# The start offsets of four activation tiles in SBUF

## The reference

```
first block:  x += fox_mixer(rms(x));  x += relu(rms(x) @ up)^2 @ down      (up 1024x4096)
              k, v from rms(x);        x += mla_mixer(rms(x));  x += the same kind of MLP
              x = rms(x)
second block: x += gla_mixer(rms(x));  x += (silu(conv(a)) * conv(u)) @ down  (up 1024x5632)
              x += short_conv_mixer(rms(x));  x += the same kind of MLP
              x = rms(x)
```

## Time and profile before

| | |
|---|---|
| median of 3 runs | 1177.66 us |
| profiled execution | 1179.46 us, span 1177.6 us |
| PE busy | 1161.7 us, 99% |
| PE weight loads busy | 1136.7 us, 97% |
| DVE, ACT, POOL busy | 866.8, 651.6, 267.0 us |
| HBM | 172 GB/s over the span |

### The profile page before, as it was taken

The page is one execution under the profiler, slowest core; times in us unless marked ns, Lnnn a source line. Parts: engine busy times, 40 slices in busy tenths (PEclk is TensorE's granted clock), DMA queues, the critical chain, the costliest instruction groups (busy, mean ns, idle before and its releaser), DMA issues.

```text
span 1177.6 us, 26235 instructions
## 1 busy us (share of the span) xinstructions
PE 1161.7 (99%) x9706; PEld 1136.7 (97%) x9706; DVE 866.8 (74%) x1387; ACT 651.6 (55%) x1075; POOL 267.0 (23%) x256
## 2 busy tenths in 40 slices
PE   9999999999999999999999999999999999999997
PEld 8998999999987999999999999999999999999997
DVE  6866777656696877755577488898768778999854
ACT  6656556544446555644555556666555455666543
POOL 0001400012230600011200263444321025444421
PEclk9999999999999999999999999999999999999999
DMA  9643665555652566465454255554656555565451
GB/s 304 194 143 108 191 194 185 180 185 171 161 162 82 179 187 200 158 205 180 142 186 157 95 168 171 189 182 147 196 188 208 190 180 179 180 201 181 146 197 59
DMA packets 213136, 203.51 MB, mean 173 GB/s; under 512 B 11840, under 2 KB 212800, under 8 KB 213072
## 3 DMA queue, kind: packets, MB, share of 16 engines
q1 hardware_dynamic: 212928, 202.44, 53.5%
q10 hardware_dynamic: 144, 0.20, 0.1%
HBM read 201.57 MB, written 1.05 MB: 172 GB/s over the span
## 4 chain that ended last, share of the span: by engine, by line
PE 94%; DVE 3%; ACT 1%; issue 1%; DMA 0%; POOL 0%; DVEq 0%; ACTq 0%; SPq 0%; POOLq 0%
PE gemm L712 28%; PE gemm L713 28%; PE gemm L714 28%; PE gemm L723 2%; PE gemm L724 1%; PE gemm L725 1%; DVE w_lo L1609 1%; PE score L905 1%; PE score L1024 1%; DMA x<-in_xT 0%; ACT w_hi L1237 0%; PE misc L750 0%; PE score L1027 0%; ACT act_a L1255 0%; PE score L1127 0%
## 5 line engine op out<-in xcount | busy, mean ns | idle before, releaser
L1609 DVE TENSOR_TENSOR w_lo<-w_raw,w_hi 128x1024 fp32r<-128x1024 f32 (+2 forms) x404 | 481.4, 1196 | 159.2 <-ACT w_hi L1237 157.4
L1237 ACT CAST w_hi<-w_raw 128x1024 fp32r<-128x1024 f32 (+2 forms) x404 | 401.5, 999 | 162.1 <-PE gemm L714 154.4
L712 PE MATMUL gemm<-act_a,w_hi 128*128 128x256 f32 (+1 forms) x1704 | 479.5, 281 | 1.4 <-DVE w_lo L1609 1.0
L713 PE MATMUL gemm<-act_a,w_hi 128*128 128x256 f32 (+1 forms) x1704 | 476.4, 280 | 0.0
L714 PE MATMUL gemm<-act_a,w_lo 128*128 128x256 f32 (+1 forms) x1704 | 475.0, 279 | 0.0
L712 PEld LDWEIGHTS gemm<-act_a,w_hi 128*128 128x128 f32 (+1 forms) x1704 | 318.7, 187 | 6.0 <-DVE w_lo L1609 2.3
L713 PEld LDWEIGHTS gemm<-act_a,w_hi 128*128 128x128 f32 (+1 forms) x1704 | 318.8, 187 | 0.4
L714 PEld LDWEIGHTS gemm<-act_a,w_lo 128*128 128x128 f32 (+1 forms) x1704 | 318.8, 187 | 0.4
L712 PE MATMUL gemm<-hid,w_hi 128*128 128x256 f32 x864 | 241.8, 280 | 0.0
L713 PE MATMUL gemm<-hid,w_hi 128*128 128x256 f32 x864 | 241.3, 279 | 0.0
L714 PE MATMUL gemm<-hid,w_lo 128*128 128x256 f32 x864 | 240.9, 279 | 0.0
(11 more groups left out here) (273 smaller groups left out, 1391.2 us busy)
## 6 DMA issues: line engine op xcount, KB each, us to landing
w_raw<-in_ffn_w_up SPq DMA_DIRECT2D x76, 1024.0 KB, 5.2
w_raw<-in_ffn_w_down SPq DMA_DIRECT2D x32, 1024.0 KB, 4.9
w_raw<-in_gla_w_in SPq DMA_DIRECT2D x12, 1024.0 KB, 5.3
w_raw<-in_ffn_w_down SPq DMA_DIRECT2D x16, 768.0 KB, 4.3
w_raw<-in_sc_w_in SPq DMA_DIRECT2D x12, 1024.0 KB, 5.2
w_raw<-in_fox_w_in SPq DMA_DIRECT2D x10, 1024.0 KB, 6.8
w_raw<-in_ffn_w_down SPq DMA_DIRECT2D x16, 640.0 KB, 3.9
w_raw<-in_fox_w_out SPq DMA_DIRECT2D x4, 1024.0 KB, 4.8
```

Source lines behind the costliest of these rows:

```text
L712: nc.tensor.matmul(ps, wh[:, k, cols], act[:, k0 + k, 0, :], start=start and k == 0, stop=False)
L713: nc.tensor.matmul(ps, wh[:, k, cols], act[:, k0 + k, 1, :], start=False, stop=False)
L1237: nc.scalar.copy(split_half(w_hi, nc_, nj), raw_half(nc_, nj)).then_inc(w_hi_ready, 1)
L1609: nc.vector.tensor_tensor(split_half(w_lo, nc_, nj), raw_half(nc_, nj), split_half(w_hi, nc_, nj).bitcast(F32), ALU.subtract).then_inc(w_l ...
```

## The change

`split_tiles` gets the offset past a multiple of 128 as an argument. The part of it that is a multiple of 32 is reached by the running address, the rest by a first part of the row that stays unused.

```diff
-        def split_tiles(name, n):
+        def split_tiles(name, n, past):
             start = used[0]
-            used[0] += (32 - start) % 128
-            return sb(name, [P, n, 2, T], F32R)
+            used[0] += (past // 32 * 32 - start) % 128
+            skip = past % 32 // 4
+            return sb(name, [P, skip + n * 2 * T], F32R)[:, skip:].rearrange("p (n s t) -> p n s t", s=2, t=T)
...
-        act_a = split_tiles("act_a", KD)
-        act_b = split_tiles("act_b", KD)
+        act_a = split_tiles("act_a", KD, past=120)
+        act_b = split_tiles("act_b", KD, past=64)
...
-        hid = split_tiles("hid", DFF // P)
+        hid = split_tiles("hid", DFF // P, past=104)
...
-        m_act = split_tiles("m_act", 5)
+        m_act = split_tiles("m_act", 5, past=40)
```

## The result

The changed kernel takes 1202.71 us (median of 4 runs, 1201.01 to 1203.60) against 1177.41 (4 runs): ratio 1.0192, 95% interval 1.0169 to 1.0215. It is 25 us slower; the forecast was 3.6 us faster, and the range ended at 1186.

What follows compares the result with a forecast made beforehand. TensorE's matmul start rate was taken to bound the kernel. From the 1177.66 us median, 3.6 us for slow stretches turning quick was subtracted, all other terms 0, giving 1174.1 us; own range 1171 to 1175, 8-in-10 range 1164 to 1186.

Steps and rivals of the forecast that it cites:

- step 2: Matmuls streaming the four moved tiles: new offsets change how stream and load meet; rate stays within 116.7 to 117.8 ns.
- rival D: Slower: act_a and hid at 118.5 ns or more while act_b, at 64, stays at 116.7; chance 0.13.
- Step 3: Slow stretches U0, CU0, CD0, SI, SO, some GQK: 3240 matmuls go from 117.8 to 116.7 ns, gaining 3.6 us.
- third rate: Gate product with 16 weight columns per load: about 115.6 ns, taken as the pace of a 256-column moving stream alone.
- rival B: Streams never meet, every full-load matmul goes to 115.6 ns: 13.2 us gained, 1164.5 us; chance 0.11 for it or a part.
- Step 4: FV and GV, 384 matmuls with the tile stationary: taken as 0, with 0.5 us either way kept for the range.
- Steps 1, 5 and 6: Instruction issue, ACT/DVE/POOL writes to shifted rows, and moved buffers behind act_a: each 0; 1.2 us for writes kept in range.
- Rival C: Everything locks to the slow rate in U1, D1, CU1, CD1, D0: 6.0 us lost, 1183.7 us; chance 0.15 with parts.
- Rival A: No change: PE's restart after a pause, not addresses, picks the rate, as hid shows both; 1177.7 us, chance 0.25.

Runs made afterwards that it cites:

- e1: TensorE's stream alone, no full kernel: moving operand's start swept 0 to 124 bytes in steps of 4, also 16-column loads, moved weights; full loads 113.9 (at 112) to 123.3 ns (at 4).
- e11: TensorE's stream alone: moving operand swept 0 to 248 bytes past the weights in steps of 8, plus pairs with both moved; 113.3 ns at 192, 113.4 at 112, 120.0 at 0.
- e2: Changed kernel with act_a at 112 for 120, hid at 96 for 104, m_act at 32 for 40: 1168.92 us, ratio 0.9913 to the kernel before.
- e3: Changed kernel with all four tiles at 64 past a multiple of 128: 1177.12 us, ratio 0.9986 to the kernel before.
- e7: Changed kernel with only hid's offset kept at 104, the other three set to 32: 1188.66 us, ratio 1.0088 to the kernel before.
- e8: TensorE's stream alone: nine starts, each entered in six ways by 1 to 6 small matmuls; 116.7 ns at 32, 117.8 at 64, two rates at 16, 104 and 120.
- e10: Changed kernel with act_a at 120, the other three at 32 modulo 256 from the weights: 1198.53 us, ratio 1.0170 to the kernel before.

## Why the prediction was wrong, point by point

- What bounds the kernel was right: TensorE's pace alone. The 24.1 us add up from distances between starts, and ACT, DVE and POOL cost nothing (L1256 508 ns as L1255 before, L1617 420, L1619 691 against 680; on POOL L634 fell from 984 to 805).
- That the load and the two streams' position to each other set the price was right and is shown, for weights at multiples of 32: at start 0 the distance is 120.0 with 128 columns of weights and 113.3 with 16 (e1), and moving both streams together keeps it (e11). That they meet in the memory is a reading; no run looks inside. "TensorE: Matmul & The Clock Gate" of the Trainium skill, in the step on LDWEIGHTS, says that loading the next weights takes no read bandwidth from the running matmul. By that rule the size of the load would make no difference; here it makes 6.7 ns at start 0 and none at start 32 (116.7 both times).
- **The step that failed is step 2**, "I stay with the rates that full loads show". It let the offset choose only between 116.7 and 117.8, the two rates of one place. Other places have other rates: 113.3, 117.1, 118.7, 120.0, 122.2. The trace had one position in 256 bytes, so it could not price another, and the nearest row above, 1.1 ns, was taken as an end although nothing made it one; rival D, which went further, got a chance of 0.13. act_a cost 2.2 to 5.5 ns more in its long stages (CU0 and SI 117.8 to 120.0, CU1 116.7 to 120.0, U0 117.8 to 122.2, U1 116.7 to 122.2).
- Step 3's sum of 3.6 us rested on step 2 and fell with it: no stage went to 116.7.
- The stream alone was put at 115.6. Its floor is 113.3 (16 columns at 0; full loads at 112 and 192), and at 32 the smaller load gains nothing (116.7 with 16 columns too). The trace of before had already shown it. The earlier trace rows are of FG; the second product with 16 columns, GA, has the same tile at the same place:

```profile
582.34 0.28 PE L712 MATMUL gemm<-act_a,w_hi 128*16 128x256 f32 x1
...
584.68 0.28 PE L714 MATMUL gemm<-act_a,w_lo 128*16 128x256 f32 x1
```

That is (584.68 - 582.34) / 20 = 117.0 ns, no quicker than full loads. So the third rate was no measure of the stream alone, and rival B's price rested on one of two such products, the one that suited it.

- "32 past a multiple of 128" hid the weights' own place, 128 past a multiple of 256. I worked out w_hi's address and checked it against 128 alone.
- Step 4: FV and GV moved by 0.3 us, inside its 0.5. Steps 1, 5 and 6 held.
- Rival D had the marks: act_a and hid slow, act_b quick (though at 113.4 where it said 116.7). It put 1.8 ns on 7860 matmuls, 14.2 us; act_a and hid cost 25.7 us. Its rule is the 16-byte lines of the Trainium skill ("SBUF — State Buffer", "Specifications (TRN2)"). The runs agree with it in part: in e11 every start 8 past a multiple of 16 ran at 119.2 or more, in e1 the one at 8 ran at 117.8. But the multiples of 16 reach from 113.3 to 120.0, and moving hid from 104 to 96 gained nothing (e2), so the crossing is not the whole cause. Rival C's place and price were those of the wrong pair of rates.
- Rival A's row was a true observation, that one address shows two rates, and e3, e7, e8 and e10 show it again; it is an effect of 1 to 5 ns on top of the place's.

Open: why 112 is good, and 192 at times, what chooses between two rates of one place, and why CU0 took 120.0 in the changed kernel and 122.2 in e10.

## What to carry to other kernels

Where TensorE is always busy, compare the distance between starts with the columns at the granted clock (106.7 ns here); the mean duration of a matmul (281 ns before, 287 after on the first product) says little of it. fp32r products of 256 columns with 128 columns of weights depend on where the tile stands to the weights modulo 256, for weights at multiples of 32: place both, and check the place by a sweep of TensorE's stream alone. With weights at 0 the sweeps gave one of the kernels' rates at each place, to 0.2 ns, but at 32, 64 and 192 not the other one. Prefer a place that showed a single rate in kernels too, as 112 did. An experiment that moves one tile moves all behind it, so list every tile's address before reading it.

## What the runs showed of the hardware that was not expected

- 256 fp32r columns never kept a steady distance below 113.3 ns at clock 1.00, 6.6 ns above one column per cycle; with 512 columns 226.7 at start 0 and 233.3 at 32 and 96 (e1).
- Starts 4 past a multiple of 16 were the slowest as a group, 120.0 to 123.3 ns; those 12 past one ran at 117.0 to 120.0 (e1).
- One place had up to three rates: 16 past the weights ran at 116.7 in e1 and e11, and at 113.3 or 118.7 in e8.
- 113.3, 116.7, 117.8, 120.0 and 122.2 ns recur in kernels and sweeps alike.
